# Scores of the sliding attention made with the keys stationary, in a two-layer hybrid trunk on one core

## What is computed

```python
def swa_sink_attention(q, k, v, sinks):
    ...
    s = jnp.einsum('bcqhgd,bckhd->bchgqk', qc, kb, preferred_element_type=F32) * (D ** -0.5)
    s = jnp.where(valid[None, :, None, None, None, :], s, -jnp.inf)
    sink = sinks.astype(F32).reshape(1, 1, Hkv, G, 1, 1)
    m = jnp.maximum(jnp.max(s, axis=-1, keepdims=True), sink)
    e = jnp.exp(s - m)
    p = e / (jnp.sum(e, axis=-1, keepdims=True) + jnp.exp(sink - m))
    out = jnp.einsum('bchgqk,bckhd->bcqhgd', p.astype(v.dtype), vb)
```

## Time and profile before

| | |
|---|---|
| runs | 2260.76, 2261.44, 2262.36 us |
| median | 2261.44 us |
| profiled execution | 2261.36 us, span from first to last instruction 2259.6 us |
| TensorE matmuls busy | 2227.7 us, 99% of the span |
| VectorE, ScalarE, GpSimd busy | 1761.6, 1183.0, 840.1 us |
| transposes of the first group and of the last | at 1441.41 and 1591.98 us |

### The profile page before, as it was taken

The page is one execution under the profiler, slowest core; times in us unless marked ns, Lnnn a source line. Parts: engine busy times, 40 slices in busy tenths (PEclk is TensorE's granted clock), DMA queues, the critical chain, the costliest instruction groups (busy, mean ns, idle before and its releaser), DMA issues. The chain is left out here.

```text
span 2259.6 us, 31830 instructions
## 1 busy us (share of the span) xinstructions
PE 2227.7 (99%) x11331; PEld 1885.4 (83%) x11331; DVE 1761.6 (78%) x2696; ACT 1183.0 (52%) x1951; POOL 840.1 (37%) x750
## 2 busy tenths in 40 slices
PE   7999999999999999999999999999999999999999
PEld 6888889999888888888888888888888888888887
DVE  5886789956557888888799767756598888888987
ACT  5658888766433444444445644655444444444454
POOL 3113346310001677777400022222048777871000
PEclk9999999999999999999999999999999999999999
DMA  5111100100322122222663542411322222228435
GB/s 169 36 50 47 34 33 29 39 1 1 140 103 75 66 84 84 84 84 84 222 216 103 181 139 61 107 39 57 112 66 84 84 84 82 82 70 303 154 118 199
DMA packets 190504, 215.18 MB, mean 95 GB/s; under 512 B 15524, under 2 KB 136708, under 8 KB 190348
## 3 DMA queue, kind: packets, MB, share of 16 engines
q1 hardware_dynamic: 185052, 195.81, 27.3%
q10 hardware_dynamic: 5296, 17.34, 2.0%
HBM read 170.77 MB, written 39.98 MB: 93 GB/s over the span
## 5 line engine op out<-in xcount | busy, mean ns | idle before, releaser
L123 PE MATMUL trunk_ps<-l_bhi,l_ahi 128*128 128x512 f32 x528 | 206.0, 390 | 0.5 <-DVE l_blo L3082 0.4
L123 PE MATMUL trunk_ps<-l_bhi,l_alo 128*128 128x512 f32 x528 | 205.5, 389 | 0.0
L123 PE MATMUL trunk_ps<-l_blo,l_ahi 128*128 128x512 f32 x528 | 205.4, 389 | 0.0
L123 PE MATMUL trunk_ps<-l_t_hi,l_s_hi 128*128 128x512 f32 x456 | 177.4, 389 | 0.0
L123 PE MATMUL trunk_ps<-l_t_hi,l_s_lo 128*128 128x512 f32 x456 | 177.4, 389 | 0.0
L123 PE MATMUL trunk_ps<-l_t_lo,l_s_hi 128*128 128x512 f32 x456 | 177.4, 389 | 0.0
L2698 POOL TENSOR_TENSOR l_s_lo<-l_raw,l_s_hi 128x512 fp32r<-128x512 f32 x90 | 158.1, 1765 | 45.5 <-ACT l_s_hi L2607 45.5
L2476 ACT ACTIVATE l_ahi<-l_a 128x512 fp32r<-128x512 f32 x132 | 83.2, 631 | 159.7 <-PE trunk_ps L123 151.2
L2698 POOL TENSOR_TENSOR l_s_lo<-l_w_sum,l_s_hi 128x512 fp32r<-128x512 f32 x76 | 120.4, 1586 | 56.6 <-ACT l_s_hi L2607 56.4
L216 POOL TENSOR_TENSOR wring_w_lo<-wring_raw,wring_w_hi 128x256 fp32r<-128x256 f32 x72 | 56.6, 817 | 191.8 <-ACT wring_w_hi L211 191.8
L123 PE MATMUL trunk_ps<-rest_hi,l_s_hi 128*128 128x512 f32 x304 | 118.3, 389 | 0.0
(11 more groups left out here) (495 smaller groups left out, 6722.6 us busy)
## 6 DMA issues: line engine op xcount, KB each, us to landing
l_draw<-in_ffn_w_out SPq DMA_DIRECT2D x154, 256.0 KB, 2.8
l_raw<-in_ffn_w_in SPq DMA_DIRECT2D x48, 512.0 KB, 4.6
gated_dram<-l_gate_out SPq DMA_DIRECT2D x44, 512.0 KB, 2.6
l_a<-gated_dram SPq DMA_DIRECT2D x88, 256.0 KB, 4.2
wring_raw<-in_even_w_in SPq DMA_DIRECT2D x20, 512.0 KB, 3.9
l_raw_g<-in_ffn_w_in SPq DMA_DIRECT2D x20, 512.0 KB, 3.9
l_raw_v<-in_ffn_w_in SPq DMA_DIRECT2D x20, 512.0 KB, 4.9
l_wt<-in_ffn_w_out SPq DMA_DIRECT2D x22, 256.0 KB, 6.0
```

The lines of the kernel that those rows point to most:

```text
L123: mm = pe.matmul(o, w, m, start=a, stop=z, skip_group_check=onto)
```

## The change

For each group the maximum is still found from queries-stationary scores, but these are now made with `k_hi` alone (4 matmuls instead of 8), three slots ahead instead of one. The scores that are used are made a second time, turned: `turned_scores(n)` has the keys stationary and all four pairs' queries (512 columns) moving, one matmul against `k_hi` and one of 65 rows against `k_lo`. The 65th row of `k_lo` is a row of ones, and the 65th row of the moving tile `shifted` is the shift, minus the larger of the maximum and eight times the sink. ScalarE then makes one exponential of 128x512 straight from PSUM into `pT`; the transposes, the copy and the four exponentials are gone.

The moving tile `shifted` (four buffers) has to be made: GpSimd copies the high halves of the group's queries into its rows 0 to 63 (`copy_queries`, two copies of 64x256), and SyncE moves the shift, which lies down a column of 128 partitions, into that 65th row with four DMAs of 128 single elements to a group (`move_shift`). These stand in SyncE's queue behind the output weights and the gains: groups 0 to 10 ahead of the first load of the residual rows, then four groups ahead of each later one. GpSimd's low rests of the weights and its roots, which ran in order by themselves, are now spread over the slots between the copies. The low rests of the keys are made once instead of twice. A definition of unused semaphores in another stage goes too; it issues nothing.

```diff
     HI_IN = {1: (0,), 2: (1,), 3: (2,), 4: (3,), 5: (4, 5), 6: (6, 7)}
     LO_IN = {2: 0, 4: 2, 6: 4, 7: 6}
+    POOL_LO = {2: 1, 4: 3, 5: 5, 6: 7}
...
-        self.prob = [at(f"prob{i}", [P, self.PAIRS, P], F32, W + 2 * KB * i) for i in range(2)]
...
+        self.shifted = [at(f"shifted{i}", [P, self.PAIRS * P], F32R, a) for i, a in enumerate((W, W + 2 * KB, fm_at + 8 * KB, fm_at + 10 * KB))]
...
-        self.S, self.TR = ([ps[i][:, HALF * h:HALF * h + HALF] for h in range(2)] for i in (0, 1))
+        self.S, self.ST = ([ps[i][:, HALF * h:HALF * h + HALF] for h in range(2)] for i in (0, 1))
...
+    def group_queries(self, n):
+        kv, c = self.where(n)
+        return self.qp[:, c // 8, c % 2, self.PAIRS * kv:self.PAIRS * kv + self.PAIRS, c // 2 % 4]
...
+        def move_shift(n):
+            sp.wait_ge(self.shift_ready, n + 1)
+            if n >= 4:
+                sp.wait_ge(self.ST_ready, n - 3)
+            for u in range(self.PAIRS):
+                sp.dma_start(self.shifted[n % 4][HD:HD + 1, u * P:u * P + P].bitcast(F32), self.shift[:, n % self.ROWS, u:u + 1].bitcast(F32),
+                             allow_slow_non_contiguous=True).then_inc(self.shift_in[n % 4], 16)
+
         for b in range(TB):
+            for n in range(4 * b + 7 if b else 0, min(4 * b + 11, self.NG)):
+                move_shift(n)
             if b == 0:
                 sp.wait_ge(self.rope_done, len(self.ROPED))
...
         def exp(n):
             nk = self.keys_of(self.where(n)[1])
-            sc.wait_ge(self.nb_ready, n + 1)
-            if n >= 2:
-                sc.wait_ge(self.T_ready, n - 1)
-            for u in range(self.PAIRS):
-                ins = sc.activation(self.prob[n % 2][:, u, 0:nk], self.S[n % 2][:, u * P:u * P + nk], ACT.Exp,
-                                    bias=self.nbias[:, n % self.ROWS, u:u + 1], scale=0.125)
-            ins.then_inc(self.exp_done, 1)
-
-        def copy(n):
-            nk = self.keys_of(self.where(n)[1])
-            sc.wait_ge(self.T_ready, n + 1)
+            sc.wait_ge(self.ST_ready, n + 1)
             if n >= 2:
                 sc.wait_ge(self.O_ready, n - 1)
-            sc.activation(self.pT[n % 2][0:nk].rearrange("p a b -> p (a b)"), self.TR[n % 2][0:nk, :], ACT.Copy).then_inc(self.copied, 1)
+            sc.activation(self.pT[n % 2][0:nk].rearrange("p a b -> p (a b)"), self.ST[n % 2][0:nk, :], ACT.Exp, scale=0.125).then_inc(self.exp_done, 1)
...
-        exp(0)
         pack_queries(N_V - 1)
-        exp(1)
         take(N_V)
         for n in range(self.LAST_SLOT):
-            if 1 <= n < NG - 1:
-                exp(n + 1)
             if n < NG:
-                copy(n)
+                exp(n)
                 sink_exp(n)
...
+        pool.wait_ge(self.cleared, 2)
+        for kv in range(2):
+            pool.tensor_copy(self.k_lo[kv][HD:HD + 1, :], self.g.const[HD:HD + 1, K_ONE:K_ONE + 1].to_broadcast([1, T])).then_inc(self.key_one, 1)
+        pool.wait_ge(self.key_one, 2)
...
+        def copy_queries(n):
+            if n == 0:
+                pool.wait_ge(self.prod_done, self.N_V)
+                pool.wait_ge(self.q_hi, 16)
+            if n == 2:
+                pool.wait_ge(self.q_lo, 32)
+            if n >= 4:
+                pool.wait_ge(self.ST_ready, n - 3)
+            out, x = self.shifted[n % 4][0:HD, :].rearrange("p (u s q) -> p u s q", u=self.PAIRS, s=2), self.group_queries(n)
+            for r in range(2):
+                pool.tensor_copy(out[:, :, r, :], x[HD * r:HD * r + HD, :, r, :].bitcast(F32)).then_inc(self.copy_ready, 1)
+                pool.wait_ge(self.copy_ready, 2 * n + r + 1)
+
+        def low_weights(k):
             pool.wait_ge(self.m_hi, k + 1)
             for c in range(0, D, D // 4):
                 w = slice(c, c + D // 4)
                 lo = pool.tensor_tensor(self.mlo[k][:, w], self.mraw[k][:, w], self.mhi[k][:, w].bitcast(F32), ALU.subtract)
             lo.then_inc(self.m_lo[1], 1)
-        for b in range(self.BY_POOL):
-            for i, squared, ready in ((0, self.sq1, self.iv1), (1, self.sq2, self.iv2)):
-                pool.wait_ge(squared, b + 1)
-                self.rsqrt(pool, i, b, ready)
+            pool.wait_ge(self.m_lo[1], k // 2 + 1)
+
+        def root(b, i):
+            pool.wait_ge((self.sq1, self.sq2)[i], b + 1)
+            self.rsqrt(pool, i, b, (self.iv1, self.iv2)[i])
+            pool.wait_ge((self.iv1, self.iv2)[i], b + 1)
+
+        pool.wait_ge(self.lo_done, self.N_ALL - self.EARLY)
+        copy_queries(0)
+        copy_queries(1)
+        pool.wait_ge(self.rope_done, len(self.ROPED))
+        pool.memset(self.v_even[:, :, :, HD:VW], 1.0).then_inc(self.ones_set, 1)
+        pool.memset(self.v_odd[:, :, :, HD:VW], 1.0).then_inc(self.ones_set, 1)
+        pool.wait_ge(self.ones_set, 2)
+        copy_queries(2)
+        for n in range(self.LAST_SLOT):
+            if n + 3 < self.NG:
+                copy_queries(n + 3)
+            if n in self.POOL_LO:
+                low_weights(self.POOL_LO[n])
+            b, i = divmod(n - 9, 4)
+            if 0 <= b < self.BY_POOL and i < 2:
+                root(b, i)
...
-                pe.wait_ge(self.key_lo, 4)
+                pe.wait_ge(self.key_hi, 4)
                 pe.wait_ge(self.q_lo, 16)
             if n == 2:
                 pe.wait_ge(self.q_lo, 32)
             if n >= 2:
-                pe.wait_ge(self.exp_done, n - 1)
+                pe.wait_ge(self.mx_ready, n - 1)
             for u in range(self.PAIRS):
                 out = self.S[n % 2][:, u * P:u * P + self.keys_of(c)]
-                queries = self.queries_of(self.PAIRS * kv + u, c)
-                pe.matmul(out, queries, self.k_hi[kv][:, self.window(c)], start=True, stop=False)
-                mm = pe.matmul(out, queries, self.k_lo[kv][:, self.window(c)], start=False, stop=True)
+                mm = pe.matmul(out, self.queries_of(self.PAIRS * kv + u, c), self.k_hi[kv][:, self.window(c)], start=True, stop=True)
             mm.then_inc(self.S_ready, 1)
 
-        def turn(n):
-            nk = self.keys_of(self.where(n)[1])
-            pe.wait_ge(self.exp_done, n + 1)
+        def turned_scores(n):
+            kv, c = self.where(n)
+            nk, keys = self.keys_of(c), self.window(c)
             if n == 0:
                 pe.wait_ge(self.taken, N_ALL)
+                pe.wait_ge(self.key_lo, 2)
+                pe.wait_ge(self.key_one, 2)
             if n >= 2:
-                pe.wait_ge(self.copied, n - 1)
-            for u in range(self.PAIRS):
-                mm = pe.transpose(self.TR[n % 2][0:nk, u * P:(u + 1) * P], self.prob[n % 2][:, u, 0:nk], ident)
-            mm.then_inc(self.T_ready, 1)
+                pe.wait_ge(self.exp_done, n - 1)
+            out = self.ST[n % 2][0:nk, :]
+            pe.matmul(out.rearrange("p (u s q) -> p u s q", u=self.PAIRS, s=2), self.k_hi[kv][:, keys], self.group_queries(n), start=True, stop=False)
+            pe.wait_ge(self.copy_ready, 2 * n + 2)
+            pe.wait_ge(self.shift_in[n % 4], 64 * (n // 4 + 1))
+            pe.matmul(out, self.k_lo[kv][0:HD + 1, keys], self.shifted[n % 4][0:HD + 1, :], start=False, stop=True).then_inc(self.ST_ready, 1)
 
         def values(n):
             kv, c = self.where(n)
             nk = self.keys_of(c)
-            pe.wait_ge(self.copied, n + 1)
+            pe.wait_ge(self.exp_done, n + 1)
             if n == 0:
...
-            if 2 <= n < NG - 1:
-                scores(n + 1)
+            if n + 3 < NG:
+                scores(n + 3)
             if n < NG:
-                turn(n)
+                turned_scores(n)
...
-                for r in range(2):
-                    dve.tensor_tensor(self.k_lo[kv][HD * r:HD * r + HD, :], self.dest(N_KEY)[own, :], self.k_hi[kv][own, :].bitcast(F32),
-                                      ALU.subtract).then_inc(self.key_lo, 1)
+                dve.tensor_tensor(self.k_lo[kv][0:HD, :], self.dest(N_KEY)[own, :], self.k_hi[kv][own, :].bitcast(F32),
+                                  ALU.subtract).then_inc(self.key_lo, 1)
...
-            dve.scalar_tensor_tensor(out=self.nbias[:, n % self.ROWS, :], in0=self.mx[:, n % self.ROWS, :], scalar=-0.125,
-                                     in1=self.nsink[:, self.PAIRS * kv:self.PAIRS * kv + self.PAIRS], op0=ALU.mult, op1=ALU.min).then_inc(self.nb_ready, 1)
-            dve.wait_ge(self.nb_ready, n + 1)
+            row, pairs = n % self.ROWS, slice(self.PAIRS * kv, self.PAIRS * kv + self.PAIRS)
             if n >= self.ROWS:
+                dve.wait_ge(self.ST_ready, n - self.ROWS + 1)
                 dve.wait_ge(self.es_done, n - self.ROWS + 1)
-            dve.tensor_tensor(self.arg[:, n % self.ROWS, :], self.nbias[:, n % self.ROWS, :],
-                              self.nsink[:, self.PAIRS * kv:self.PAIRS * kv + self.PAIRS], ALU.subtract).then_inc(self.arg_ready, 1)
```

(14 more changed lines are left out.)

26 lines of the change are left out of this document (13 added, 13 removed).

## The result

The changed kernel takes 2285.3 us (median of 4, 2284.5 to 2287.5), the kernel before beside it 2261.1 us (median of 4): a ratio of 1.0109, 95% interval 1.0094 to 1.0124. Slower, as forecast, but by 24 us instead of 9, just above the range. The profiled execution took 2285.15 us.

A forecast was written before the change was run, and what follows sets the result against it. TensorE was taken as the bound. The first output projection comes 19.0 us later and the slots behind it gain 10.3: net +8.7 on 2261.36, so 2270.1 us, range 2262 to 2283.

The forecast's parts named there:

- The bound, and a wait paid in full: TensorE, matmuls busy 99% of the span, bounds the kernel; removed work is gained, a wait on it paid in full.
- The stall: At the attention's start, TensorE idles about 20 us before group 0's second turned matmul, its shift queued behind weights and gains.
- The release, 1462.0: Group 0's shift lands and frees its second turned matmul at about 1462.0, just behind the second gain at 1461.4.
- some 0.6 for themselves: Time for group 0's shift transfers themselves, after the second gain has landed: some 0.6 us.
- The third rival: Single-element shift transfers are themselves slow, up to 5.1 us a group: 2292 us; chance 0.11 for all beyond 2280.
- The clock, 1.2 us: After the idle gap TensorE restarts at low clock, slowing some eight 512-column matmuls: 0 to 1.6 us, taken as 1.2.
- The dense slots, 10.3 us: From slot 5's projection on, fewer score matmuls less dearer turned matmuls: 10.3 us gained, slots about 5.0 instead of 5.40.
- GpSimd at nothing: GpSimd's query copies, up to 1.5 us a slot, cost nothing, with up to 2 us for late roots or low weights.
- Everything 0.9 earlier: Scores of groups 0 and 1 inside the last projection lose four matmuls each, so everything behind starts 0.9 us earlier.
- The case's range: Range of the main forecast alone, 2265 to 2279 us, with chance 0.65.
- the full range: Whole prediction's range, 2262 to 2283 us, leaving out the second rival and the slow tail.

The follow-up runs named there:

- the first experiment: Changed kernel with shift moves of groups 0 and 1 ahead of the output weights in SyncE's queue, each further group's behind one weight tile: 2260.0 us, ratio 0.9994.

## Why the prediction was right in kind and wrong in size

- **The bound, and a wait paid in full**: right. From slot 31 to the end the two kernels take the same (667.6 and 667.9 us).
- **The stall**: right in place and cause. First shift issued at 1448.72 (forecast 1448.9), landings 14 us, idle 23.2 us before the matmul it named. Weight loads took 10.13 us to issue, as read. Once the queue was empty four moves took 2.4 us (forecast 2.6); the issues slowed to about 1 us each while it was backed up, which cost nothing more, since the landings decided.
- **The release, 1462.0**: the first step that failed. It came at 1467.08. The term "some 0.6 for themselves" for single elements was about 5 us (4 to 6 in three profiles): with whole rows or runs of 16 bytes the release is at 1462.6 and 1461.8. What the prediction quotes from the Trainium skill, "DMA: Bandwidth & Descriptors" (it stands under Rules for kernel authors), one descriptor per element, agrees with the trace: the twenty moves of 1468 to 1490 made 2880 packets under 512 B. The third rival, slow element transfers, was thus partly true, for the groups that pile up in the queue; singly they land in 2 us, and in dense slots they cost nothing.
- **The clock, 1.2 us**: the largest miss. Slots 0 to 5 were priced at 10.9 us from the release to the first projection and took 17.5, with no wait in them. The clock accounts for it: in the profile with three more matmuls to a slot and the clock at 1.00, the same stretch took 14.95 us, with 15 added matmuls of 0.21 us and 1.64 us of waits, so about 10 without them (an estimate). The working took the number of slow matmuls at the kernel's start, eight of them, where dense work follows, as if the clock came back after as many here. These slots are full of short matmuls, and the change itself takes matmuls out of them. That removing work can lower the clock was in no step, nor in any rival.
- **The dense slots, 10.3 us**: the slot is 5.01 us, as forecast, but from the first projection on only 7.5 us came. Slot 5 still ran at half clock (0.95 lost). Slots 7 and 9 hardly gained, 5.35 and 5.54 us where they were 5.41 and 5.56: one waits for a weight's low part, the other for ScalarE. Every fourth slot has 5.11 to 5.13 us, also slot 29, which holds no scores any more and should have had about 4.5.
- **GpSimd at nothing**: right; its copies take 0.40 us each and TensorE waits for none from slot 6 on.
- **"Everything 0.9 earlier"**: right for the last projection and the weights' issue, both 1.1 us earlier, wrong for the groups. TensorE waits 1.82 us for the packed queries instead of 0.29, so group 0's turned matmul was at 1443.44, later than the old transposes at 1441.41. Behind the stall it costs nothing; in the first experiment it does.

The sum: 8.7 forecast, + 5.1 release, + 6.6 clock, + 2.8 dense slots = 23.2; the spans differ by 23.3. The case's range went up to 2279, with 4 us for the clock and GpSimd and 4 for the elements, each short of its own miss; the full range, to 2283, still fell short of all three together.

## What to carry to other kernels

Before a small transfer is put in front of a busy engine, read what stands ahead of it on its queue, both in issuing and in bytes: here the same 512 bytes took 2 or 14 us. Then ask of work that is taken out of a thin stage whether the clock still holds without it: here half clock took part of the freed time, and matmuls whose result was thrown away held the clock at 1.00 at a cost of under 1 us, but in time they gained nothing either. The gain in the dense part, 8.5 us, was real; it was the start of the stage, some 20 us in the kernel before, that decided the sign.

## What the runs showed of the hardware that was not expected

- A 512-column matmul that contracts 64 rows, between ones of 128, costs 0.4 us more than one of 65 rows.
- A moving operand read with a step of 8 or 16 bytes makes a 512-column fp32 matmul 0.62 us instead of 0.40. GpSimd's copies with such a destination took 0.41 us (8 bytes) and 0.64 (16) instead of 0.40.
- A 512 KB load whose outer dimension is 2 moves at 52 GB/s.
- Sixteen moves of single elements, queued behind a 512 KB load, put off that load's own landing: 15.1 to 18.0 us in three profiles, 12.2 to 13.4 without such moves.
- SyncE's issuing slows behind a full queue: 3.2 us for a move in place of 0.6, behind the loads at 52 GB/s.
- In stages of short matmuls the granted clock falls to 0.50 with TensorE at work, behind waits of 0.8 to 1 us and in one profile with none over 0.12 us, and in the profiles with 512-column matmuls added to the same slots it doesn't. A wait of 1.95 us once left it at 1.00, one of 1.82 us didn't. Where exactly it turns was not measured.
